# First expert's rows by one-hot products instead of an indirect transfer and transposes

## The chip, the cores and the metric

One core of one Trainium2 chip runs the whole program. The metric is the device time of one execution in microseconds (us). The kernel before takes 1440.48 us, the median of three runs (1439.84 to 1441.86).

## The reference, cut to what matters

Two layers of an encoder over 512 tokens of width 1024, all in float32. In each layer a token mixer (layer 0: convolution and a linear recurrence; layer 1: sliding-window attention) is followed by a mixture of experts: 16 experts, of which each token takes two, and each expert is a gated network of width 512.

```python
h = modulate(rmsnorm(x, norm_ffn_g[l]), sh2, sc2)        # per channel: scale and shift
x = x + g2[:, None, :] * grouped_moe(h, router_w, router_bias, ...)

# grouped_moe: sigmoid scores, best group of four experts, top two in it;
# the tokens of each expert are laid into blocks of 128 rows, absent rows are zero
xs = hpad[slot_tok].reshape(n_blocks, DISPATCH_BLOCK, D)
yb = (silu(xb @ w_gate[e]) * (xb @ w_up[e])) @ w_down[e]  # for every block
out = zeros.at[slot_tok].add(yb * slot_w[:, None])
```

## The kernel before, in words

The layer's tokens stand as four tiles of 128 rows. `experts(l)`, which each engine has in its own version, does the whole mixture of layer l. In the order of time:

**Routing.** For each tile the residual is added, the rows are normalized (`xnorm[s]`, 128 tokens by 1024 channels, kept in SBUF: `mod_ring` in layer 0, `x_norm` in layer 1, since s = 2l + 1), ScalarE's queue stores them to the DRAM tensor `xn_rows` (L818), and logits, scores and choices follow (`choose`). TensorE then counts ranks (L1740, L1742). From these VectorE makes the places:

- `place_first` (L1281 to L1291): the place of each token in expert 0's block, as a one-hot `first_hot` (128 tokens by 128 places, four tiles). TensorE multiplies it with a column of token numbers (L1747) and VectorE turns the sum into the first column of `slot_tok`, the list of the tokens of each block.
- `route` (L1293 to L1327): the same for all other blocks, by a chain of small VectorE instructions, eight products on TensorE (L1752) and two instructions for the remaining columns of `slot_tok` (L1325, L1326).

**Gathers.** GpSimd's queue fetches each block's rows from `xn_rows` by an indirect transfer into one of two buffers `xs` (L637 for experts 0 and 1, L644 for the others, always two experts ahead; the buffer is free when `xs_turned` has counted its transposes).

**Expert 0's entry.** `turn_xs` makes eight transposes of 128x128 into PSUM banks 0 and 1 (L1757); the stride in the gathered rows puts channels kt, kt + 8, ... on the partitions. `xst` takes them out with the layer's scale and shift, half on ScalarE (L833, L836), half on VectorE (L1401, L1404), and splits them into a high and a low part (VectorE, L1407).

**The expert loop.** For each expert TensorE makes 24 gate products (`split_product`, L1771: high times high, high times low and low times high part of the weights, 128x512 in fp32r, three for each of eight slices), the down product of the expert before (L1782, plain f32), the transposes of the next expert's rows (L1757), and 24 up products (L1771). Meanwhile ScalarE copies the high part of the weights (`high`, L804), VectorE subtracts it for the low part (`low`, L1377), and SyncE's queue refills the weight buffers (`refill`), each as soon as `gate_done`, `up_done` or `down_done` frees it. Weights come in slabs of 2 MB; two experts' slabs are loaded ahead of the loop. Blocks beyond the sixteenth, from experts with more than 128 tokens, run after the loop in the same way but one after the other (L1762).

Order is written out by hand: every engine runs its instructions in the order of its program, and semaphores order the engines. On VectorE the order is `place_first`, `route`, `xst(0)`, the low part of expert 0's up weights, `route_rest` (information for the extra blocks, combine weights), the low part of expert 1's gate weights, `xst(1)`. On TensorE it is L1747, L1752, the transposes of expert 0, its gate products, the transposes of expert 1 (L1813, behind a wait for `xs_filled[1]`), its up products. The gate weights of expert 0 are split during routing.

Of the kernel before, what the change touches and what calls it, by code (L numbers as in the profile page):

```python
# [92 lines left out]
def build(nc, ctx, a, out):  # L93
    def small(name, shape, dt=F32):
        return ctx.enter_context(nc.sbuf_tensor(name, shape, dt))
# [54 lines left out]
    first_hot = R_r[:, 12, :].rearrange("p (t n) -> p t n", n=P)  # L150
# [31 lines left out]
    tok_pair = small("token_id_pair", [P, TT, 2], F32R)  # L182
# [71 lines left out]
    xs_turned, xst_act, xst_dve = sem("xs_turned"), sem("xst_act"), sem("xst_dve")  # L254
    high_ready, low_ready = [sem("gate_high"), sem("up_high")], [sem("gate_low"), sem("up_low")]
# [82 lines left out]
    LAST = 4 * 7 + AV_LAG  # L338
    QK_BANK = [0, 1, 2, 3, 4, 5, 0, 1] + [2, 4, 5, 6, 7, 6, 7, 6]
# [242 lines left out]
    def _(gp):  # L582
# [46 lines left out]
        def gathers(l):  # L629
# [3 lines left out]
            gp.wait_ge(slots_ready, 2 * l + 1)  # L633
# [14 lines left out]
            gather_first(0, xs_filled[0])  # L648
            gp.wait_ge(slots_ready, 2 * l + 2)
# [51 lines left out]
    def _(act):  # L701
# [93 lines left out]
        def experts(l):  # L795
# [29 lines left out]
            def xst(e, par, first=False):  # L825

                if not first:
                    act.wait_ge(up_done, e + (e0 - 1))
                if first and par:
                    act.wait_ge(route_ready, l + 1)  # L830
                act.wait_ge(xs_turned, e + (e0 + 1))
                for kt in range(4):
                    ins = act.activation(xsT[par][:, kt, :], ps[:, 0, kt * P:(kt + 1) * P], ACT.Identity, bias=AB[:, s, 1, kt:kt + 1], scale=AB[:, s, 0, kt:kt + 1])  # L833
                ins.then_inc(xst_act, 1)
                act.wait_ge(xst_act, e + (e0 + 1))
                act.activation(xs_high[l][par][:, 0:4, :], xsT[par][:, 0:4, :], ACT.Copy).then_inc(xs_high_ready, 1)  # L836
# [124 lines left out]
    def _(v):  # L961
# [277 lines left out]
        link(v.tensor_copy(tok_pair[:, :, :], tok1[:, :].unsqueeze(2).to_broadcast([P, TT, 2])))  # L1239
# [41 lines left out]
        def place_first(l):  # L1281
# [5 lines left out]
            v.wait_ge(slots_summed, 2 * l + 1)  # L1287
            found = ps[:, 2, 0:1]
            link(ts(empty[:, 0:1], found, 0.0, float(NO_TOKEN), ALU.is_equal, ALU.mult))
            stt(slot_tok[:, 0:1], found, -1.0, empty[:, 0:1], ALU.add, ALU.add).then_inc(slots_ready, 1)  # L1290
            v.wait_ge(slots_ready, 2 * l + 1)  # L1291

        def route(l):  # L1293
# [29 lines left out]
            v.wait_ge(slots_summed, 2 * l + 2)  # L1323
            slots = ps[:, 2, 1:WIDE]
            link(ts(empty[:, 1:WIDE], slots, 0.0, float(NO_TOKEN), ALU.is_equal, ALU.mult))  # L1325
            stt(slot_tok[:, 1:WIDE], slots, -1.0, empty[:, 1:WIDE], ALU.add, ALU.add).then_inc(slots_ready, 1)  # L1326
            v.wait_ge(slots_ready, 2 * l + 2)  # L1327
# [21 lines left out]
        def experts(l):  # L1349
# [46 lines left out]
            def xst(e, par, first=False):  # L1396
                if not first:
                    v.wait_ge(up_done, e + (e0 - 1))
                v.wait_ge(xs_turned, e + (e0 + 1))
                for kt in range(4, KT):  # L1400
                    ins = ts(xsT[par][:, kt, :], ps[:, 1, (kt - 4) * P:(kt - 3) * P], AB[:, s, 0, kt:kt + 1], AB[:, s, 1, kt:kt + 1], ALU.mult, ALU.add)  # L1401
# [35 lines left out]
            xst(0, 0, True)  # L1437
            step(0, 0, first=True)
# [159 lines left out]
    def _(pe):  # L1598
# [106 lines left out]
        def experts(l):  # L1705
# [40 lines left out]
            for t in range(TT):  # L1746
                ins = pe.matmul(ps[:, 2, 0:2], first_hot[:, t, :], tok_pair[:, t, :], start=(t == 0), stop=(t == TT - 1))  # L1747
            ins.then_inc(slots_summed, 1)

            pe.wait_ge(place_ready, 2 * l + 2)  # L1750
            for i in range(2 * TT):
                ins = pe.matmul(ps[:, 2, 0:WIDE], place_hot[:, i, :], block_tok[:, i, :], start=(i == 0), stop=(i == 2 * TT - 1))  # L1752
# [43 lines left out]
            def step(e, par, turn, first=0, last=False):  # L1796
# [13 lines left out]
                if not last:  # L1810

                    pe.wait_ge(xs_filled[1 - par], (turn + par) * 16 + (16 + (NE // 2) * l * 16))
                    turn_xs(1 - par, xs_turned)  # L1813
# [3 lines left out]
            pe.wait_ge(xs_filled[0], (NE // 2) * l * 16 + 16)  # L1817
            turn_xs(0, xs_turned)
# [166 lines left out]
```

## Time and profile before

| | us |
|---|---|
| median of 3 runs | 1440.48 |
| the profiled execution | 1440.28 |
| its span | 1438.5 |
| TensorE (PE) busy | 1267.1 (88%) |
| VectorE (DVE) busy | 945.9 (66%) |
| ScalarE (ACT) busy | 592.0 (41%) |
| GpSimd (POOL) busy | 169.3 (12%) |

Mean granted TensorE clock 0.945 of 2.4 GHz; it has two levels, 1.00 (2.4 GHz) and 0.50 (1.2 GHz). Expert 0's first product starts at about 316 us in layer 0 and at about 1034 us in layer 1. The span is the time on the core from the first to the last instruction; the execution's own time is 1.8 us longer. Times of rows are counted from the start of the span. Matmuls are pipelined and their ends are modelled: the time that one costs in a row of many is the distance of the starts, not its own duration. PEld is the load of the stationary operand, DVEq or POOLq an engine's sequencer. In a chain of waits each piece is what released the next.

### The profile page before, as it was taken

The page shows a single profiled execution, that of the slowest core. Times are in us where ns is not written, and L with a number is a line of the kernel's source. Part 1 is how long each engine was busy: PE and PEld are TensorE (multiplying, and loading weights), DVE is VectorE, ACT ScalarE, POOL GpSimd, SP SyncE. Part 2 cuts the span into 40 slices and gives each one's busy share as a digit, 9 for nine tenths or more (in the row PEclk, how much of TensorE's full clock was granted, in tenths as well). Part 3 has the DMA queues.
Part 4 walks back from the last instruction along what each step waited for, and adds up shares of the span by engine and source line. Part 5 has one row for each costly group of instructions (what it writes and reads, how often), then busy time and mean ns, then how long its engine had stood idle before and what let it go on. Part 6 is the DMA issues. An engine that isn't in the chain of part 4 may idle for free.

```text
span 1438.5 us, 14181 instructions
## 1 busy us (share of the span) xinstructions
PE 1267.1 (88%) x4821; PEld 813.9 (57%) x4821; DVE 945.9 (66%) x1336; ACT 592.0 (41%) x774; POOL 169.3 (12%) x177
## 2 busy tenths in 40 slices
PE   2979899948999999983899999999489999999881
PEld 2434344546666667741788854467466666667430
DVE  8468985566777777713866588856667777777114
ACT  3246200335555555502422157734255555554001
POOL 6100000010000000002000047710110000000002
PEclk9999999959999999997899999999599999999996
DMA  9984575047999999883375230023679999998445
GB/s 354 375 283 124 198 256 212 30 146 273 372 363 369 373 372 375 307 334 122 127 282 185 88 117 1 1 74 127 241 289 374 377 366 365 378 363 310 146 181 190
DMA packets 79615, 353.12 MB, mean 245 GB/s; under 512 B 12696, under 2 KB 12880, under 8 KB 70608
## 3 DMA queue, kind: packets, MB, share of 16 engines
q1 hardware_dynamic: 67680, 327.28, 61.7%
q0 software_dynamic: 8352, 20.46, 3.9%
q10 hardware_dynamic: 3536, 4.79, 0.9%
q8 instruction: 26, 0.43, 0.1%
q14 instruction: 21, 0.17, 0.0%
HBM read 334.15 MB, written 28.31 MB: 252 GB/s over the span
## 4 chain that ended last, share of the span: by engine, by line
PE 74%; DVE 12%; SPq 5%; DMA 4%; ACT 2%; issue 2%; POOL 1%; DVEq 0%; ACTq 0%; POOLq 0%
PE ps L1771 24%; PE ps L1782 17%; PE ps L1870 8%; PE ps L1691 4%; PE ps L1762 3%; PE ps L1658 3%; PE ps L1698 2%; PE ps L1757 2%; DVE scratch L974 2%; PE ps L1914 2%; PE ps L1942 2%; SPq L398 2%; PE ps L1928 2%; DMA mod_ring<-in_mod_w_dram 1%; PE ps L1621 1%
## 5 line engine op out<-in xcount | busy, mean ns | idle before, releaser
L1782 PE MATMUL ps<-slab_ring,scratch 128*128 128x512 f32 x560 | 246.5, 593 | 3.4 <-ACT scratch L882 2.1
L1771 PE MATMUL ps<-slab_ring_r,gate_rows_r 128*128 128x512 f32 x512 | 202.4, 395 | 0.0
L1782 PEld LDWEIGHTS ps<-slab_ring,scratch 128*128 128x128 f32 x560 | 105.8, 190 | 124.2 <-issue 117.3
L1377 DVE TENSOR_TENSOR slab_ring_r<-slab_ring,h_t_r 128x2048 fp32r<-128x2048 f32 x64 | 143.9, 2287 | 17.2 <-ACT h_t_r L804 17.1
L1658 PE MATMUL ps<-h_t,slab_ring 128*128 128x512 f32 x320 | 141.2, 600 | 0.0
L1870 PE MATMUL ps<-slab_ring_r 128*128 128x512 f32 x384 | 121.2, 397 | 2.7 <-DVE h_t_r L1031 2.7
L1771 PE MATMUL ps<-h_t_r,gate_rows_r 128*128 128x512 f32 x256 | 106.4, 415 | 14.8 <-DVE scratch_r L1407 7.6
L804 ACT ACTIVATE h_t_r<-slab_ring 128x2048 fp32r<-128x2048 f32 x64 | 118.6, 1901 | 0.0
L1771 PEld LDWEIGHTS ps<-slab_ring_r,gate_rows_r 128*128 128x128 f32 x512 | 98.4, 192 | 19.4 <-issue 0.5
L1658 PEld LDWEIGHTS ps<-h_t,slab_ring 128*128 128x128 f32 x320 | 61.8, 194 | 77.8 <-issue 77.2
L833 ACT ACTIVATE scratch<-ps,mod_ab 128x128 f32<-128x128 f32 x128 | 48.1, 456 | 136.0 <-PE ps L1757 136.0
L1771 PE MATMUL ps<-h_t_r,scratch_r 128*128 128x512 f32 x256 | 103.0, 402 | 0.0
L1377 DVE TENSOR_TENSOR slab_ring_r<-slab_ring,x_norm_r 128x2048 fp32r<-128x2048 f32 x32 | 73.2, 2292 | 42.1 <-ACT x_norm_r L804 42.1
L1377 DVE TENSOR_TENSOR slab_ring_r<-slab_ring,mod_ring_r 128x2048 fp32r<-128x2048 f32 x32 | 73.2, 2292 | 41.3 <-ACT mod_ring_r L804 41.3
L696 POOL TENSOR_SCALAR mod_ring<-mod_ring,row_rcp 128x512 f32<-128x512 f32 x48 | 76.9, 1614 | 185.5 <-DVE row_rcp L1554 185.4
L1870 PEld LDWEIGHTS ps<-slab_ring_r 128*128 128x128 f32 x384 | 72.6, 190 | 20.0 <-issue 2.9
L1411 DVE TENSOR_TENSOR scratch<-ps,gate_rows 128x512 f32<-128x512 f32 x70 | 45.1, 686 | 53.9 <-PE ps L1782 52.9
L804 ACT ACTIVATE mod_ring_r<-slab_ring 128x2048 fp32r<-128x2048 f32 x32 | 61.1, 1912 | 46.8 <-PE ps L1771 46.6
L804 ACT ACTIVATE x_norm_r<-slab_ring 128x2048 fp32r<-128x2048 f32 x32 | 61.1, 1911 | 46.8 <-PE ps L1771 46.6
L1870 PE MATMUL ps<-slab_ring_r,h_t_r 128*128 128x512 f32 x192 | 75.3, 392 | 0.0
L1771 PEld LDWEIGHTS ps<-h_t_r,gate_rows_r 128*128 128x128 f32 x256 | 50.1, 196 | 25.8 <-issue 16.4
L974 DVE SCALAR_TENSOR_TENSOR scratch<-slab_ring,c_silu,scratch 128x1024 f32<-128x1024 f32 x42 | 59.9, 1426 | 3.9 <-DMA slab_ring<-in_mod_w_dram 2.6
(318 smaller groups left out, 2065.2 us busy)
## 6 DMA issues: line engine op xcount, KB each, us to landing
slab_ring<-in_expert_w_gate_dram SPq DMA_DIRECT2D x35, 2048.0 KB, 10.0
slab_ring<-in_expert_w_up_dram SPq DMA_DIRECT2D x35, 2048.0 KB, 10.4
slab_ring<-in_expert_w_down_dram SPq DMA_DIRECT2D x35, 2048.0 KB, 10.4
mod_ring<-in_mod_w_dram SPq DMA_DIRECT2D x48, 512.0 KB, 4.6
y_rows<-scratch SPq DMA_DIRECT2D x35, 512.0 KB, 10.8
slab_ring<-in_mod_w_dram SPq DMA_DIRECT2D x32, 512.0 KB, 4.6
slab_ring<-in_w_qkv_dram SPq DMA_DIRECT2D x6, 2048.0 KB, 11.3
slab_ring<-in_w_in_ab_dram SPq DMA_DIRECT2D x5, 2048.0 KB, 18.0
```

The source lines that it names most:

```text
L696: gp.tensor_scalar(prob[n % 8], prob[n % 8], rsum[:, n:n + 1], None, ALU.mult).then_inc(scaled_pool, 1)
L804: act.activation(top, w, ACT.Copy).then_inc(high_ready[c], 1)
L833: ins = act.activation(xsT[par][:, kt, :], ps[:, 0, kt * P:(kt + 1) * P], ACT.Identity, bias=AB[:, s, 1, kt:kt + 1], scale=AB[:, s, 0, kt: ...
L974: ins = stt(dest, w, cs[:, m:m + 1], dest, ALU.mult, ALU.add)
L1377: tt_(rest, w, top.bitcast(F32), ALU.subtract).then_inc(low_ready[c], 1)
L1411: ins = tt_(buf[:, h * HALF:h * HALF + HALF], ps[:, 5 + h, :], G[:, 2 * l + 1, h * HALF:h * HALF + HALF], ALU.mult)
L1658: ins = pe.matmul(ps[:, z_bank(t), :], slab(("in", g))[:, kt, j * P:(j + 1) * P], HT[:, kt, :], start=(kt == 0), stop=(kt == KT - 1))
L1691: ins = pe.matmul(ps[:, 2 * t + half, :], mixT[:, kt, cut], slab(("out", half))[:, kt, :], start=(i == 0), stop=(i == KT - 1))
L1762: ins = pe.matmul(ps[:, bank, :], xsT[0][:, kt, :], w[:, kt, :], start=(kt == 0), stop=(kt == KT - 1))
L1771: ins = pe.matmul(ps[:, bank, :], x, w, start=(kt == 0 and i == 0), stop=(kt == KT - 1 and i == 2))
L1782: ins = pe.matmul(ps[:, 5 + h, :], hidT[:, f, :], w[:, 2 * f + h, :], start=(f == 0), stop=(f == FT - 1))
L1870: ins = pe.matmul(ps[:, i % 6, :], x[:, kt, cut], y[:, k, :], start=(kt == 0 and n == 0), stop=(kt == KT - 1 and n == 2))
```

## The change

The rows of expert 0, already transposed, are made by products of the normalized rows with the one-hot of places: for each of the eight slices of channels four products (one for each tile of tokens, summed in PSUM), 32 in all, into banks 4 and 5. The stationary operand is `xnorm[s][:, t, kt:D:KT]`, with a stride of 8 elements, the moving one `first_hot[:, t, :]`. The indirect transfer and the eight transposes for expert 0 are gone, and so are the first column of the slots, its four products and VectorE's two instructions for it. `first_hot` is f32 instead of fp32r. The 32 products stand on TensorE where the four were, ahead of the eight slot products, which now go to bank 3. `xst` of expert 0 waits for `first_rows`, ScalarE's half after 16 products and VectorE's after 32. The two instructions that form the other columns of `slot_tok`, with their wait, move on VectorE from the end of `route` to behind `xst(0)` (`find_slots`); the gather of expert 1 waits for them. As `turn_xs(0)` is gone, TensorE raises `xs_turned` by itself once after the slot products, so that the gather of expert 2 into `xs[0]` may follow.

```diff
--- before.py
+++ after.py
@@ -147,7 +147,7 @@
     block_tok = R_r[:, 11, 0:2 * TT * WIDE].rearrange("p (a b) -> p a b", b=WIDE)
     XT = [R[:, 8 + 2 * i:10 + 2 * i, :].rearrange("p a (b n) -> p (a b) n", n=P) for i in range(2)]
     rw_scaled, rw_shift = (R[:, 12, i * P:(i + 1) * P].rearrange("p (k e) -> p k e", e=NE) for i in range(2))
-    first_hot = R_r[:, 12, :].rearrange("p (t n) -> p t n", n=P)
+    first_hot = R[:, 12, :].rearrange("p (t n) -> p t n", n=P)
     comb = [[XN[:, t, :] for t in range(TT)],
             [modr[:, 2 * t:2 * t + 2, :].rearrange("p a n -> p (a n)") for t in range(TT)]]
 
@@ -630,7 +631,7 @@
             e0 = l * NE
             gp.wait_ge(xn_ready, 4 * (2 * l + 2))
             link(gp.memset(R[:, 0:4, :], 0.0))
-            gp.wait_ge(slots_ready, 2 * l + 1)
+            gp.wait_ge(slots_ready, l + 1)
             gp.wait_ge(xn_stored, 16 * TT * (l + 1))
 
             def gather_first(buf, done):
@@ -645,8 +646,6 @@
                                       in_offset=bass.IndirectOffsetOnAxis(ap=idx[buf][:, 0:1], axis=0),
                                       bounds_check=S - 1, oob_is_err=False).then_inc(done, 16)
 
-            gather_first(0, xs_filled[0])
-            gp.wait_ge(slots_ready, 2 * l + 2)
             gather_first(1, xs_filled[1])
             with gp.Fori(0, NE // 2 - 1) as i:
                 link.enter_loop(i, 0, 2)
@@ -828,9 +827,13 @@
                     act.wait_ge(up_done, e + (e0 - 1))
                 if first and par:
                     act.wait_ge(route_ready, l + 1)
-                act.wait_ge(xs_turned, e + (e0 + 1))
+                if first and not par:
+                    act.wait_ge(first_rows, 2 * l + 1)
+                else:
+                    act.wait_ge(xs_turned, e + (e0 + 1))
+                bank = FIRST_BANK if first and not par else 0
                 for kt in range(4):
-                    ins = act.activation(xsT[par][:, kt, :], ps[:, 0, kt * P:(kt + 1) * P], ACT.Identity, bias=AB[:, s, 1, kt:kt + 1], scale=AB[:, s, 0, kt:kt + 1])
+                    ins = act.activation(xsT[par][:, kt, :], ps[:, bank, kt * P:(kt + 1) * P], ACT.Identity, bias=AB[:, s, 1, kt:kt + 1], scale=AB[:, s, 0, kt:kt + 1])
                 ins.then_inc(xst_act, 1)
                 act.wait_ge(xst_act, e + (e0 + 1))
                 act.activation(xs_high[l][par][:, 0:4, :], xsT[par][:, 0:4, :], ACT.Copy).then_inc(xs_high_ready, 1)
@@ -1284,11 +1286,6 @@
             link(stt(first_rank[:, :], hot[:, :, 0], -float(PAST), v3(ps[:, 1, 0:n])[:, :, 0], ALU.mult, ALU.add))
             link(ts(first_rank[:, :], first_rank[:, :], float(PAST), None, ALU.add))
             tt_(first_hot, p_id[:, :].unsqueeze(1).to_broadcast([P, TT, P]), first_rank[:, :].unsqueeze(2).to_broadcast([P, TT, P]), ALU.is_equal).then_inc(place_ready, 1)
-            v.wait_ge(slots_summed, 2 * l + 1)
-            found = ps[:, 2, 0:1]
-            link(ts(empty[:, 0:1], found, 0.0, float(NO_TOKEN), ALU.is_equal, ALU.mult))
-            stt(slot_tok[:, 0:1], found, -1.0, empty[:, 0:1], ALU.add, ALU.add).then_inc(slots_ready, 1)
-            v.wait_ge(slots_ready, 2 * l + 1)
 
         def route(l):
 
@@ -1320,11 +1317,14 @@
                 ins = tt_(block_tok[:, j * TT:(j + 1) * TT, :], at[:, j * TT:(j + 1) * TT, :], tok1[:, :].unsqueeze(2).to_broadcast([P, TT, WIDE]), ALU.mult)
             ins.then_inc(place_ready, 1)
             v.wait_ge(place_ready, 2 * l + 2)
-            v.wait_ge(slots_summed, 2 * l + 2)
-            slots = ps[:, 2, 1:WIDE]
+
+        def find_slots(l):
+
+            v.wait_ge(slots_summed, l + 1)
+            slots = ps[:, SLOT_BANK, 1:WIDE]
             link(ts(empty[:, 1:WIDE], slots, 0.0, float(NO_TOKEN), ALU.is_equal, ALU.mult))
             stt(slot_tok[:, 1:WIDE], slots, -1.0, empty[:, 1:WIDE], ALU.add, ALU.add).then_inc(slots_ready, 1)
-            v.wait_ge(slots_ready, 2 * l + 2)
+            v.wait_ge(slots_ready, l + 1)
 
         def route_rest(l):
 
@@ -1396,9 +1396,14 @@
             def xst(e, par, first=False):
                 if not first:
                     v.wait_ge(up_done, e + (e0 - 1))
-                v.wait_ge(xs_turned, e + (e0 + 1))
+                bank = 1
+                if first and not par:
+                    bank = FIRST_BANK + 1
+                    v.wait_ge(first_rows, 2 * l + 2)
+                else:
+                    v.wait_ge(xs_turned, e + (e0 + 1))
                 for kt in range(4, KT):
-                    ins = ts(xsT[par][:, kt, :], ps[:, 1, (kt - 4) * P:(kt - 3) * P], AB[:, s, 0, kt:kt + 1], AB[:, s, 1, kt:kt + 1], ALU.mult, ALU.add)
+                    ins = ts(xsT[par][:, kt, :], ps[:, bank, (kt - 4) * P:(kt - 3) * P], AB[:, s, 0, kt:kt + 1], AB[:, s, 1, kt:kt + 1], ALU.mult, ALU.add)
                 ins.then_inc(xst_turned, 1)
                 v.wait_ge(xst_turned, e + (e0 + 1))
                 v.tensor_copy(xs_high[l][par][:, 4:8, :], xsT[par][:, 4:8, :]).then_inc(xst_split, 1)
@@ -1435,6 +1440,7 @@
                 tt_(hid, ps[:, 3, :], sg, ALU.mult).then_inc(hid_ready, 1)
 
             xst(0, 0, True)
+            find_slots(l)
             step(0, 0, first=True)
             step(1, 1)
             step(2, 0)
@@ -1743,13 +1749,17 @@
             ins.then_inc(rank_ready, 1)
 
             pe.wait_ge(place_ready, 2 * l + 1)
-            for t in range(TT):
-                ins = pe.matmul(ps[:, 2, 0:2], first_hot[:, t, :], tok_pair[:, t, :], start=(t == 0), stop=(t == TT - 1))
-            ins.then_inc(slots_summed, 1)
+            pe.wait_ge(xn_ready, TT * s + TT)
+            for kt in range(KT):
+                for t in range(TT):
+                    ins = pe.matmul(ps[:, FIRST_BANK + kt // 4, (kt % 4) * P:(kt % 4 + 1) * P], xnorm[s][:, t, kt:D:KT], first_hot[:, t, :], start=(t == 0), stop=(t == TT - 1))
+                if kt == 3:
+                    ins.then_inc(first_rows, 1)
+            ins.then_inc(first_rows, 1)
 
             pe.wait_ge(place_ready, 2 * l + 2)
             for i in range(2 * TT):
-                ins = pe.matmul(ps[:, 2, 0:WIDE], place_hot[:, i, :], block_tok[:, i, :], start=(i == 0), stop=(i == 2 * TT - 1))
+                ins = pe.matmul(ps[:, SLOT_BANK, 0:WIDE], place_hot[:, i, :], block_tok[:, i, :], start=(i == 0), stop=(i == 2 * TT - 1))
             ins.then_inc(slots_summed, 1)
 
             def turn_xs(buf, done):
@@ -1809,13 +1819,15 @@
                     down_product(e - 1, 1 - par, prev_turn, first == 2)
                 if not last:
 
-                    pe.wait_ge(xs_filled[1 - par], (turn + par) * 16 + (16 + (NE // 2) * l * 16))
+                    if par == 0:
+                        pe.wait_ge(xs_filled[1], turn * 16 + (16 + (NE // 2) * l * 16))
+                    else:
+                        pe.wait_ge(xs_filled[0], turn * 16 + (16 + (NE // 2 - 1) * l * 16))
                     turn_xs(1 - par, xs_turned)
                 pe.wait_ge(low_ready[1], 2 * e + (2 * e0 + 2))
                 split_product(par, 1, 3, range(KT)).then_inc(up_done, 1)
 
-            pe.wait_ge(xs_filled[0], (NE // 2) * l * 16 + 16)
-            turn_xs(0, xs_turned)
+            pe.sem_inc(xs_turned, 1)
             step(0, 0, 0, first=1)
             step(1, 1, 0, first=2)
             with pe.Fori(1, NE // 2 - 1) as i:
```

Here `FIRST_BANK` is 4 and `SLOT_BANK` 3; `first_rows` is a new semaphore, and the tile `tok_pair` with the cast that filled it (L1239) is gone.

## Rows read from the trace of the kernel before

**Rows 1.** The page: the chain that ended last, shares by engine.
```profile
PE 74%; DVE 12%; SPq 5%; DMA 4%; ACT 2%; issue 2%; POOL 1%; DVEq 0%; ACTq 0%; POOLq 0%
```

**Rows 2.** Timeline of layer 0, 300 to 317 us: start us, us, engine, line, instruction.
```profile
301.73 1.01 PE L1747 MATMUL ps<-token_id_pair,scratch_r 128*128 128x2 f32 x4 [1.18 <-DVE scratch_r L1286]
...
303.17 0.17 DVE L1296 TENSOR_SCALAR scratch<-ps 128x16 f32<-128x16 f32 x1
...
308.81 1.88 PE L1752 MATMUL ps<-scratch_r 128*128 128x24 f32 x8 [6.06 <-DVE scratch_r L1320]
...
310.54 1.97 PE L1757 MATMUL ps<-ident,scratch 128*128 128x128 f32 x8
...
311.98 1.01 POOL L637 DMA_INDIRECT scratch<-xn_rows,slot_token  x1 [6.83 <-DVE slot_token L1326]
...
312.62 1.37 DVE L1401 TENSOR_SCALAR scratch<-ps,mod_ab 128x128 f32<-128x128 f32 x4 [1.42 <-PE ps L1757]
...
314.81 1.22 DVE L1407 TENSOR_TENSOR scratch_r<-scratch,gate_rows_r 128x1024 fp32r<-128x1024 f32 x1 [0.36 <-ACT gate_rows_r L836]
...
316.14 0.76 PE L1771 MATMUL ps<-h_t_r,gate_rows_r 128*128 128x512 f32 x1 [3.63 <-issue]
...
316.54 4.49 DVE L1377 TENSOR_TENSOR slab_ring_r<-slab_ring,x_norm_r 128x2048 fp32r<-128x2048 f32 x2 [0.51 <-ACT x_norm_r L804]
```

**Rows 3.** Chain of waits, layer 1, 1000 to 1060 us: start us, us, what.
```profile
1009.14 11.23 DMA xn_rows<-x_norm
...
1021.24 7.05 DMA scratch<-xn_rows,slot_token
...
1028.34 1.99 PE ps L1757 x8
...
1033.94 7.71 PE ps L1771 x24
```

**Rows 4.** Timeline of layer 1, the same product as at 301.73.
```profile
1016.97 1.01 PE L1747 MATMUL ps<-token_id_pair,scratch_r 128*128 128x2 f32 x4 [1.18 <-DVE scratch_r L1286]
```

**Rows 5.** Chain of waits, layer 0, 285 to 345 us: gate products of experts 0 and 1.
```profile
316.14 8.17 PE ps L1771 x24
...
334.43 4.58 PE ps L1771 x12
```

**Rows 6.** Chain of waits inside the expert loop, 345 to 600 us.
```profile
349.06 0.89 PE ps L1757 x8
349.94 8.20 PE ps L1771 x36
...
361.35 6.87 PE ps L1782 x16
```

**Rows 7.** Timeline of TensorE alone, three places: layer 0 before routing; logits; layer 1's start.
```profile
283.77 3.60 PE L1691 MATMUL ps<-slab_ring,x_norm 128*128 128x512 f32 x8
...
290.92 3.57 PE L1718 MATMUL ps<-scratch 128*128 128x16 f32 x16 [0.89 <-ACT scratch L811]
...
686.92 1.97 PE L1606 MATMUL ps<-ident,x_norm 128*128 128x128 f32 x8 [1.53 <-DVE x_norm L1010]
690.01 1.19 PE L1870 MATMUL ps<-slab_ring_r 128*128 128x512 f32 x2 [1.12 <-DVE h_t_r L1031]
```

**Rows 8.** Windows: us, busy (count) of PE, PEld, DVE, ACT, POOL, then PEclk, DMA, GB/s.
```profile
290.40:290.80 0.40, 0.00 (x0) 0.00 (x0) 0.40 (x2) 0.38 (x2) 0.00 (x0) 0.75 1.14 492
335.00:336.00 1.00, 1.00 (x4) 0.81 (x3) 1.00 (x1) 0.00 (x0) 0.00 (x0) 0.50 1.07 459
338.00:339.00 1.00, 1.00 (x6) 0.77 (x5) 0.00 (x0) 0.00 (x0) 0.00 (x0) 0.81 0.00 0
321.00:324.00 3.00, 3.00 (x14) 2.46 (x13) 2.23 (x12) 0.00 (x0) 0.00 (x0) 0.95 0.00 0
692.00:694.00 2.00, 2.00 (x8) 1.60 (x7) 1.93 (x6) 1.45 (x3) 0.00 (x0) 0.66 0.12 49
```

**Rows 9.** Landing times of the transfers that read slot_token.
```profile
DMA to landing us min/median/max: 3.4/4.6/7.1
```

More of the change, by code:

```diff
@@ L181, in build @@
     shift_row = small("router_shift_row", [P, NE])
-    tok_pair = small("token_id_pair", [P, TT, 2], F32R)
     first_rank = small("first_rank", [P, TT])
@@ L254, in build @@
     xs_turned, xst_act, xst_dve = sem("xs_turned"), sem("xst_act"), sem("xst_dve")
+    first_rows = sem("first_rows")
     high_ready, low_ready = [sem("gate_high"), sem("up_high")], [sem("gate_low"), sem("up_low")]
@@ L338, in build @@
     LAST = 4 * 7 + AV_LAG
+    FIRST_BANK, SLOT_BANK = 4, 3
     QK_BANK = [0, 1, 2, 3, 4, 5, 0, 1] + [2, 4, 5, 6, 7, 6, 7, 6]
@@ L1238, in _ @@
         n = TT * NE
-        link(v.tensor_copy(tok_pair[:, :, :], tok1[:, :].unsqueeze(2).to_broadcast([P, TT, 2])))
         sc, bia, o1, o2, t0, t1, t2, t3 = (rt[:, i * n:(i + 1) * n] for i in range(8))
```

## The prediction

> **What bounds the kernel now.** I read the page's chain first: TensorE carries 74% of it [rows 1]. In the expert loop it never pauses; every piece begins where the last one ended [rows 6]. The change leaves the loop's body alone, so it can only move the moment at which each of the two layers enters it. Next I read the timelines of both entries, from the routing to expert 0's first gate product.
>
> In layer 0 [rows 2] the one-hot of places is ready when the four products of L1747 start, at 301.73. VectorE waits for them, forms column 0 of the slots, and only at 303.17 begins `route`. The route ends with the eight slot products at 308.81; TensorE works in order, so expert 0's eight transposes follow at 310.54. They end at 312.51, VectorE takes its half at 312.62, and the gate products start at 316.14. The gather for expert 0 isn't in this: it was hidden behind the route. In layer 1 it is [rows 3]: a store of normalized rows takes 11.23 us, the gather issued behind it 7.05, and the transposes come at 1028.34, the gate products at 1033.94. The one-hot was ready at 1016.97 [rows 4].
>
> The clock matters too. Over 24 gate products TensorE needs 8.17 and 7.71 us [rows 5, 3], where 36 products in the loop take 8.20, or 0.228 each [rows 6], 5.5 for 24. So 2.7 and 2.2 us are lost to the lower clock at the two entries.
>
> **The change, part by part.**
>
> 1. Products for expert 0. Per layer 32 plain f32 products of 128x128 by 128x128 replace four products and eight transposes. No row has this form. The nearest are f32 transposes with the same strided stationary: 8 in 0.89 us, 0.111 each, at 2.4 GHz [rows 6], and 8 in 1.97, about 0.24, at 1.2 GHz [rows 7]; products with 16 columns show 16 in 3.57, 0.22 each [rows 7]. A plain f32 product of 512 columns takes 6.87/16 = 0.429 [rows 6]; a quarter of that is 0.107, no more than the transpose. I take 0.111 and 0.23. The lower bound is 0.107; the upper is a 128-column product that costs as much as a 512-column one, 0.43, and double that at half clock. The transposes are nearest, in shape and in stride, so I stay with them.
>
> 2. The clock while they run. They start at 1.2 GHz. Dense 512-column products got the full clock 5.2 us after their start (316.14 to 321.3: 0.95 granted in 321 to 324), 4.0 us (334.43 to 338.4) and 3.35 us (690.01 to 693.36) [rows 2, 5, 7, 8]. I take 4.3: 19 products in 4.3 us, 13 in 1.45, with the last one's drain 5.9 us. They end at 307.6 and 1022.9.
>
> By the Trainium skill (FP8 and Floating Point Precision, TensorE Precision Notes) true f32 is four passes through the array. The trace disagrees: its plain f32 product costs 0.429 against 0.228 for the split one, less than twice. With four passes of 128 columns at the two clocks, the products would end 3 us later in each layer.
>
> 3. VectorE without its wait. `route` starts at once, 1.44 us earlier, and ends at about 307.3 and 1022.5; TensorE's products end later, so they bind, by 0.3 us. VectorE's wait for the eight slot products disappears ahead of `xst`. They run beside `xst` and cost the path nothing; without this cover they would cost the 1.73 us between their start and that of the transposes [rows 2].
>
> 4. `xst`. Before, from the end of the transposes to the gate product, 316.14 - 312.51 = 3.63 us, of which 0.36 waits for ScalarE's copy [rows 2]. ScalarE now starts after half the products (first at about 305.5) and finishes first, so 3.27 remain. Gate products start at 310.9 and 1026.2: **5.2 and 7.7 us earlier**. All 24 gate products' other operands are ready: the low part of the gate weights is made before routing.
>
> 5. Clock at the gate products. The eight slot products end near 308.6, and 2.3 us of pause follow. The clock fell 3.2 us after the products that ended at 287.4 (three quarters granted in 290.4 to 290.8), with eight transposes between, and some 4.4 us after the end of expert 0's up products, which is 0.5 us into the next burst (0.50 in 335 to 336) [rows 7, 8]. So I expect it to fall about when the gate products start and to come back as for expert 1, whose first 12 took 4.58 us [rows 5] against 2.73: 1.85 lost instead of 2.7 and 2.2. **Gain 0.85 and 0.35.** The bounds are no fall, 2.7 and 2.2, and no gain, 0.
>
> 6. Moved: the other slots, now behind `xst`. Two small instructions, 0.4 us like column 0's pair between 302.74 and 303.17, stand ahead of the low part of the up weights. Queued behind them on VectorE are 4.49 us of that [rows 2] and the eleven small instructions of `route_rest`, by L1296's 0.17 and at most twice that some 2 to 3.5 us, so VectorE is free by 317.6 to 319.2. The next work for it, expert 1's gate weights, waits for ScalarE, which copies them only after the gate products (318.2) and its silu. Nothing is late. ScalarE makes the high part of the up weights earlier than now, so VectorE's 0.51 wait there goes too.
>
> 7. Moved: expert 1's gather. It is issued about 0.8 us after its slots, near 312, with 3.4 to 7.1 us to land [rows 9, 2], so by 319.1 at worst; TensorE wants it when the gate products end, at 318.2. Expert 1 starts 10.1 us after that (324.3 to 334.43), of which TensorE needs 1.04 for transposes and 5.5 for up products, so 3.5 us are free. Cost zero. In layer 1 it is issued at about 1027.2, as now. POOL has one indirect transfer less to issue; expert 2's can't pass expert 1's, since it stands behind it. No weight transfer moves in its order on SP; its refills follow the gate products and move with them.
>
> 8. PE's empty increment, the cast of L1239 that is gone, and f32 instead of fp32r in the one-hot: nothing, the same width is written.
>
> Sum: 5.2 + 7.7 + 0.85 + 0.35 = 14.1. The profiled execution took 1440.28 us, 0.2 less than the median 1440.48; 1440.28 - 14.1 = **1426.2**.
>
> **The rivals.**
>
> A, the clock stays high at the gate products. The pause of 2.3 us is shorter than each after which it was seen to fall. Against it: in layer 0 eight transposes in the pause didn't keep it up, and the eight slot products are as short. Both losses vanish, 2 x 1.85 = 3.7 us more: 1422.5.
>
> B, the clock doesn't rise during the 32 products. For it: 16 logit products in 3.57 us and two groups of eight transposes (the second ends at 688.9) ran at the low clock throughout [rows 7]. Against: each dense burst of true products with many columns in the rows brought it up, and the new ones run for 6 us without a pause. 32 x 0.235 = 7.5 us, gates at 312.5 and 1027.8, gain 3.6 + 6.1, nothing from the clock: 1430.6.
>
> C, load and stream don't overlap for 128 columns. 0.106 for the load (half of the logits' 0.22) and 0.107 for the stream make 0.213. 10 products in 4.3 us and 22 in 4.7 end at 310.7 and 1026.0; gates at 314.0 and 1029.2, gain 2.1 + 4.7 + 1.2 = 8.0: 1432.3. Four passes would come out at the same place.
>
> D, slower: TensorE becomes the bound of the entry, each product costing as much as one of 512 columns (item 1's upper bound). Five in 4.3 us and 27 x 0.43 = 11.6 end 16 us after the start, gates at 321.0 and 1036.2: 4.9 + 2.3 later, 1447.5. It decides from some 0.41 us a product: 11.1 and 13.7 us until the products would end as late as the path allows now, plus the clock, over 32. Every f32 row of 128 columns lies below, so it is unlikely.
>
> E, expert 1's gather lands late, as the store's 11.23 us did: at about 323.2, 1.5 us past the slack in each layer: 1429.2.
>
> That the change doesn't do what it says is small in layer 0: the transfer was hidden there, and what is gained is the wait, slots and transposes.
>
> **How the numbers follow.** Forecast 0.43, A 0.22, B 0.16, C 0.13, E 0.04, D 0.02. The range takes in A, B and C with the bounds of the clock: 1421.5 to 1433.0. About 0.2%, 2.9 us, is what a measurement of this kernel can tell from no change; all cases but D lie beyond it on the faster side. With something left for what is not seen: faster 0.95, same 0.03, slower 0.02.
>
> **What would show it.** Right: 32 products at 0.11 to 0.24 us starting at 301.7; L1296 within 0.1 us of L1286's end; the first gate product at 310 to 312 and 1025 to 1027.5; PE waiting for no transfer before expert 1; the loop's pieces unchanged (8.20 and 6.87). Wrong: a mean above 0.25 per product, a granted clock of 0.50 through all of them, a wait for the transfer into `xs[1]`, or an expert loop with pauses.

## The result and the profile after

The changed kernel takes 1449.92 us, the median of five runs (1448.04 to 1452.46), against 1441.15 us for the kernel before in the same series. The ratio is 1.0065 with a 95% interval of 1.0054 to 1.0075: **slower by 0.65%, where 1% faster was forecast**. A second series of five gave 1448.91 us and 1.0055 (1.0041 to 1.0069). In the series that timed v3 and b1, one execution of b1 and one of the kernel before took some 1740 us at a granted clock of 0.73; the ratios leave both out.

The page of the changed kernel, its busy times and its chain, beside [rows 1]:

```profile
PE 1291.1 (89%) x4925; PEld 836.9 (58%) x4925; DVE 944.4 (65%) x1331; ACT 592.6 (41%) x774; POOL 169.9 (12%) x175
...
PE 75%; DVE 12%; SPq 5%; DMA 2%; ACT 2%; issue 2%; POOL 1%; DVEq 0%; ACTq 0%; POOLq 0%
```

TensorE is 24 us busier (1267.1 before). Its timeline at layer 0's entry, the stretch that answers to [rows 2] (L1755 are the new products, L1762 the slot products, L1781 the gate products; L1288 makes the one-hot and L1293 is the first instruction of `route`):

```profile
304.09 0.69 DVE L1288 TENSOR_TENSOR scratch<-place_id,first_rank 128x512 f32<-128x512 f32 x1
304.70 0.17 DVE L1293 TENSOR_SCALAR scratch<-ps 128x16 f32<-128x16 f32 x1
...
304.84 15.54 PE L1755 MATMUL ps<-scratch,mod_ring 128*128 128x128 f32 x64 [1.18 <-DVE scratch L1288]
...
309.86 0.43 DVE L1317 TENSOR_TENSOR scratch_r<-scratch,token_id_plus 128x96 fp32r<-128x96 f32 x2
312.79 1.51 ACT L836 ACTIVATE scratch<-ps,mod_ab 128x128 f32<-128x128 f32 x4 [13.92 <-PE ps L1755]
...
320.13 1.04 PE L1762 MATMUL ps<-scratch_r 128*128 128x24 f32 x8
320.49 1.37 DVE L1406 TENSOR_SCALAR scratch<-ps,mod_ab 128x128 f32<-128x128 f32 x4 [10.20 <-PE ps L1755]
...
323.49 0.17 DVE L1325 TENSOR_SCALAR slot_empty<-ps 128x23 f32<-128x23 f32 x1
...
323.68 0.77 PE L1781 MATMUL ps<-h_t_r,gate_rows_r 128*128 128x512 f32 x1 [2.50 <-issue]
```

VectorE starts `route` at 304.70, at the moment at which the one-hot is ready, as the change meant, and ends it at 310.3. Then it stands still for 10.2 us: the 32 products run from 304.84 to 320.38. Everything behind them has the form that was forecast: the slot products in their cover, 3.30 us from the last product to the first gate product. In layer 1, the answer to [rows 3, 4], products and entry are the same to a hundredth:

```profile
1024.69 15.54 PE L1755 MATMUL ps<-scratch,x_norm 128*128 128x128 f32 x64 [1.18 <-DVE scratch L1288]
...
1043.54 0.77 PE L1781 MATMUL ps<-h_t_r,gate_rows_r 128*128 128x512 f32 x1 [2.51 <-issue]
```

The rows of line L1755 alone:

```profile
L1755 PEld LDWEIGHTS ps<-scratch,mod_ring x64: 312/336/338, 304.8 to 319.8; 128*128 128x128 f32 x64
L1755 PE MATMUL ps<-scratch,mod_ring x64: 342/402/604, 304.8 to 320.0; 128*128 128x128 f32 x64
```

The code writes 32 products a layer, and here are 64 matmuls. A plain f32 product is **two** records (rows of the trace), each with its own load. And a record costs 15.5/64 = 0.24 us whatever the clock does. The windows of the same stretch (us, busy time and count of PE, PEld, DVE, ACT, POOL, then PEclk, DMA, GB/s; a count takes in the records that a window's edge cuts, so it is higher than the window's length over the price of one):

```profile
306.00:308.00 2.00, 2.00 (x10) 2.00 (x10) 1.73 (x9) 0.00 (x0) 0.00 (x0) 0.50 0.00 0
308.00:310.00 2.00, 2.00 (x11) 2.00 (x10) 1.90 (x4) 0.00 (x0) 0.00 (x0) 0.79 0.00 0
318.00:320.00 2.00, 2.00 (x10) 2.00 (x10) 0.00 (x0) 1.84 (x2) 0.00 (x0) 1.00 0.00 0
320.00:321.00 1.00, 1.00 (x10) 1.00 (x9) 0.51 (x2) 0.00 (x0) 0.00 (x0) 1.00 0.00 0
322.00:323.00 1.00, 0.00 (x0) 0.00 (x0) 0.97 (x2) 0.00 (x0) 0.00 (x0) 0.75 0.00 0
323.00:324.00 1.00, 0.32 (x1) 0.35 (x2) 0.93 (x4) 0.00 (x0) 0.00 (x0) 0.50 0.00 0
```

The granted clock rises at 308.8 (0.79 over 308 to 310), 4.0 us after the start, and the ten records in each 2 us don't become more. The slot products right behind, plain records of 24 columns, run at some 0.11 us each. The clock falls at 322.5 (0.75 over 322 to 323), 1.3 us after the last slot product, while VectorE takes the rows out, so that the gate products begin at the lower clock again. In the chain they take 8.36 us; expert 1 follows at its old distance (316.14 to 334.43 before was 18.3, now 18.5):

```profile
323.68 8.36 PE ps L1781 x24
...
342.16 3.06 PE ps L1781 x8
```

The table has, for the kernels of this study except the control b1, the records that make expert 0's rows in a layer, the way from the first of them to the first gate product ("entry"), and from there to the transposes of expert 1 ("gate"), for layer 0 / layer 1, read from the starts in the timelines. Times are medians, or one run where a single one is marked.

| kernel | records | entry | gate | time |
|---|---|---|---|---|
| before | 4 + 8 | 14.41 / 16.97 | 7.99 / 7.53 | 1441.15 |
| changed | 64 | 18.84 / 18.85 | 8.18 / 8.34 | 1449.92 |
| r1, changed again | 64 | 18.86 / 18.83 | 7.54 / 7.94 | 1448.91 |
| u1, slots ahead | 64 | 20.08 / 20.34 | 6.95 / 7.26 | 1448.58 |
| e1, contiguous | 64 | 12.26 / 12.97 | 7.19 / 5.78 | 1432.08, one |
| v1, permuted rows | 64 | 13.52 / 12.16 | 8.38 / 7.19 | 1437.00 |
| e4, v3, one pass | 32 | 11.24 / 11.24 | 8.00 / 7.40 | 1431.42 |
| v2, permuted, one pass | 32 | 10.39 / 10.39 | 8.31 / 7.16 | 1432.29 |
| e2, transposes | 32 | 8.71 / 8.98 | 6.69 / 5.74 | 1421.94, one |
| e3, one tile | 16 | 8.67 / 8.67 | 7.50 / 8.12 | 1427.59, one |

(The entry and gate columns of "e4, v3" are e4's; its time is v3's.) Before to changed, the entries cost 4.4 + 1.9 and the gate products 0.2 + 0.8: 7.3 us of a measured 8.8 and 8.1. The profiled execution was the slowest of its five (span 12.2 us longer): its routing in layer 0 began 3.1 us later than before, and in r1 that start lies within 0.3 us of before (301.98 against 301.73). So that part is scatter between executions.

### The profile page after: what moved, and what is told of

The parts are those of the page before. It is cut to its first block, busy times and chain, and to the rows that moved or that the text cites. A ratio compares the mean times of both kernels' runs of the same rounds, so it can differ in the third digit from the quotient of the medians.

```text
span 1450.7 us, 14377 instructions
## 1 busy us (share of the span) xinstructions
PE 1291.1 (89%) x4925; PEld 836.9 (58%) x4925; DVE 944.4 (65%) x1331; ACT 592.6 (41%) x774; POOL 169.9 (12%) x175
## 4 chain that ended last, share of the span: by engine, by line
PE 75%; DVE 12%; SPq 5%; DMA 2%; ACT 2%; issue 2%; POOL 1%; DVEq 0%; ACTq 0%; POOLq 0%
PE ps L1781 24%; PE ps L1792 17%; PE ps L1882 8%; PE ps L1697 4%; PE ps L1772 3%; PE ps L1664 3%; PE ps L1704 2%; PE ps L1755 2%; DVE scratch L977 2%; SPq L399 2%; PE ps L1767 2%; PE ps L1926 2%; PE ps L1954 2%; PE ps L1940 2%; PE ps L1627 1%
## 5 line engine op out<-in xcount | busy, mean ns | idle before, releaser
L1781 PE MATMUL ps<-slab_ring_r,gate_rows_r 128*128 128x512 f32 x512 | 203.1, 397 | 0.0
L1377 DVE TENSOR_TENSOR slab_ring_r<-slab_ring,h_t_r 128x2048 fp32r<-128x2048 f32 x64 | 143.9, 2288 | 18.5 <-ACT h_t_r L803 18.4
L1781 PE MATMUL ps<-h_t_r,gate_rows_r 128*128 128x512 f32 x256 | 106.6, 417 | 12.6 <-DVE scratch_r L1412 7.6
L1781 PEld LDWEIGHTS ps<-slab_ring_r,gate_rows_r 128*128 128x128 f32 x512 | 98.5, 192 | 19.4 <-issue 0.5
L1781 PE MATMUL ps<-h_t_r,scratch_r 128*128 128x512 f32 x256 | 103.3, 403 | 0.0
L1781 PEld LDWEIGHTS ps<-h_t_r,gate_rows_r 128*128 128x128 f32 x256 | 50.0, 195 | 23.0 <-issue 13.5
## 6 DMA issues: line engine op xcount, KB each, us to landing
slab_ring<-in_expert_w_down_dram SPq DMA_DIRECT2D x35, 2048.0 KB, 10.2
```

The source lines that it names most:

```text
L1377: tt_(rest, w, top.bitcast(F32), ALU.subtract).then_inc(low_ready[c], 1)
L1781: ins = pe.matmul(ps[:, bank, :], x, w, start=(kt == 0 and i == 0), stop=(kt == KT - 1 and i == 2))
```

## The experiments

**e1, contiguous stationary.** Does the stride make the record dear?

```diff
-pe.matmul(..., xnorm[s][:, t, kt:D:KT], first_hot[:, t, :], ...)
+pe.matmul(..., xnorm[s][:, t, kt * P:(kt + 1) * P], first_hot[:, t, :], ...)
```

> The changed kernel with the stationary operand of the 32 products taken from 128 neighbouring columns instead of every eighth (it multiplies other channels, so expert 0's rows hold the wrong channels; the work is the same). Stride theory: each f32 product is two matmul records, and a record with a strided stationary costs 0.24 us at either clock, a contiguous one 0.23 at the low and 0.11 at the full clock; the clock rises about 4 us after the start, so the 64 records take about 9.2 us instead of 15.5, and the way from the first product to the first gate product 12.5 us instead of 18.85 in each layer, some 12 us less in all, about 1438. Rival, the stream or the accumulation of 128 columns sets the 0.24: nothing changes, 15.5 us and about 1450.

1432.08 us in one run, beside 1439.98 for the kernel before. The loads of L1755 in layer 0, and the windows around them:

```profile
L1755 PEld LDWEIGHTS ps<-scratch,mod_ring x64: 192/192/338, 303.3 to 311.9; 128*128 128x128 f32 x64
```

```profile
304.00:306.00 2.00, 2.00 (x11) 2.00 (x11) 1.76 (x8) 0.00 (x0) 0.00 (x0) 0.50 0.00 0
306.00:308.00 2.00, 2.00 (x18) 2.00 (x17) 1.83 (x6) 0.00 (x0) 0.00 (x0) 0.86 0.03 8
308.00:310.00 2.00, 2.00 (x21) 2.00 (x20) 0.70 (x3) 1.28 (x4) 0.00 (x0) 1.00 0.00 0
316.00:318.00 2.00, 2.00 (x8) 1.59 (x7) 2.00 (x1) 0.00 (x0) 1.30 (x1) 0.70 0.00 0
```

The same 64 records take 8.96 us instead of 15.54. Their load falls to 192 ns, and with the clock full a window of 2 us counts 21 records, not 10. For the products and the entry the stride theory's numbers came out (9.2 and 12.5 expected; 8.96 and 12.26 measured in layer 0, 9.66 and 12.97 in layer 1, where the clock rose later, 4.7 us after the start against 3.3); the rival, that the stream or accumulation of 128 columns sets 0.24, is refuted. The time came out 6 us below the 1438 expected. Beside r1 below, the gate products are 2.5 us shorter in all, and an extra block behind the loop takes 14.02 us instead of 15.71; neither was in the estimate, and the rest isn't resolved.

**e2, transposes.** What the prediction had priced, put in the place of the products.

```diff
-ins = pe.matmul(..., xnorm[s][:, t, kt:D:KT], first_hot[:, t, :], start=(t == 0), stop=(t == TT - 1))
+ins = pe.transpose(..., xnorm[s][:, t, kt:D:KT], ident[:, :])
```

> The changed kernel with 32 transposes (identity as the moving operand, the same strided stationary) in place of the 32 f32 products; expert 0's rows are the wrong ones. This is what the prediction priced. If the count of records was its error, there are 32 records here; at 0.11 after the clock has risen they take 5.9 us, at 0.23 throughout (earlier transposes never raised the clock) 7.5 us; the first gate product comes 9.3 to 10.8 us after the first record, and the time is 1426 to 1431. Rival, the stride costs 0.24 a record in transposes too: 7.7 us and no drop even when the clock is full.

1421.94 us in one run, 4 below what was expected at best. The loads in layer 0, then the chain behind the first gate products:

```profile
L1755 PEld LDWEIGHTS ps<-ident,mod_ring x32: 185/200/226, 303.2 to 308.2; 128*128 128x128 f32 x32
```

```profile
313.02 5.51 DMA scratch<-xn_rows,slot_token
...
318.57 1.16 PE ps L1767 x8
319.73 5.49 PE ps L1781 x24
...
327.71 2.30 PE ps L1781 x9
```

32 records, 5.41 us, with a stride and yet 0.11 each at the full clock: the same stationary operand is cheap in a transpose and dear in a true product. The entry is 8.71 us. The clock is still full at the gate products (5.74 us in layer 1; the 6.69 of layer 0 hold a wait, below), so it is the prediction's case A in its mechanism, and within a microsecond of that case's 1422.5. The chain also shows the gather of expert 1 landing after the gate products, TensorE waiting for it until 318.57, and expert 1's gate products at 327.71. That is 15.8 us after expert 0's at 311.88, and in layer 1, where nothing waited, it is 15.8 too (1018.11 to 1033.93): the wait of about a microsecond went into the slack.

**e3, one tile of four.** The dose: 16 records.

```diff
-for t in range(TT):
-    ins = pe.matmul(..., start=(t == 0), stop=(t == TT - 1))
+for t in range(1):
+    ins = pe.matmul(..., start=(t == 0), stop=True)
```

> The changed kernel with 8 products of the 32: only the first 128 tokens are looked through, so most of expert 0's rows are missing. 16 records at 0.24: 3.9 us. The products no longer bind; the first gate product comes where VectorE's route ends, about 5.4 us after the start of the products, plus 3.3 for taking the rows out, so 8.8 us instead of 18.85: 20 us less in all than the changed kernel, about 1430. If something other than these products delays the entry (code, the moved slots), it stays above 12 us.

1427.59 us in one run. Timeline of VectorE's last route instructions and what follows:

```profile
306.70 0.43 DVE L1317 TENSOR_TENSOR scratch_r<-scratch,token_id_plus 128x96 fp32r<-128x96 f32 x2
307.16 1.37 DVE L1406 TENSOR_SCALAR scratch<-ps,mod_ab 128x128 f32<-128x128 f32 x4
...
310.35 0.76 PE L1781 MATMUL ps<-h_t_r,gate_rows_r 128*128 128x512 f32 x1 [1.29 <-issue]
```

The products end before `route`, VectorE goes from L1317 straight into L1406, and the entry is 8.67 us. Nothing else in the changed entry delays it, neither code nor moved slots. The way of 8.67 us through VectorE is the floor of this order of work.

**e4, one pass.** One record a product, the stride kept. For this the normalized rows and the one-hot are written as fp32r, the type in which the split products take their operands and to which f32 values are rounded; so all experts' rows are rounded.

```diff
-first_hot = R[:, 12, :].rearrange("p (t n) -> p t n", n=P)
+first_hot = R_r[:, 12, :].rearrange("p (t n) -> p t n", n=P)
...
-ts(xnorm[s][:, t, :], X[:, t, :], r, None, ALU.mult)
+ts((xnorm_r if s % 2 else xnorm)[s][:, t, :], X[:, t, :], r, None, ALU.mult)
...
-pe.matmul(..., xnorm[s][:, t, kt:D:KT], ...)
+pe.matmul(..., xnorm_r[s][:, t, kt:D:KT], ...)
```

> The changed kernel with normalized rows and one-hot written as fp32r, so that each of the 32 products is one record instead of two; all experts' rows are rounded to fp32r. Stride theory in its strict form (0.24 for every strided true product): 32 records in 7.7 us, the first gate product 11 us after the first record instead of 18.85, about 1434. If the stride costs only in the two-record f32 form: 5.9 us, 9.3 us, about 1431. Rival (stream or accumulation of 128 columns sets it): also half of 15.5.

1431.28 us. The loads, and two of four windows, which all read alike:

```profile
L1756 PEld LDWEIGHTS ps<-scratch_r,mod_ring_r x32: 313/337/339, 302.7 to 310.1; 128*128 128x128 f32 x32
```

```profile
304.00:306.00 2.00, 2.00 (x10) 2.00 (x10) 1.72 (x9) 0.00 (x0) 0.00 (x0) 0.50 0.00 0
...
310.00:312.00 2.00, 2.00 (x11) 2.00 (x10) 1.29 (x4) 2.00 (x2) 0.00 (x0) 0.50 0.00 0
```

32 records in 7.93 us, 0.25 each: the strict form of the theory in its numbers (7.7 and 11 expected, 7.93 and 11.24 measured). The total doesn't tell the cases apart: 1434 was expected for this one, 1431 for the other. It isn't settled whether the stride holds fp32r records at 0.24 when the clock is full, as the clock never rose here.

**r1, the changed kernel again.**

> The changed kernel unaltered, on the chip and in the hour of the next three, to see how much of its 9 us belongs to the two entries. The entries are 4.4 and 1.9 us longer than before and the gate products there 0.2 and 0.6: 7.1 us. If the rest (the profiled run began layer 0's routing 3.1 us later, before anything that the change touches) is the scatter of this kernel's runs, the median stands 7 to 9 us above the kernel before; if the change delays the program's start as well, 10 to 12.

1448.91 us, 8.1 above before, with the entries as in the first profile. By the table entries and gate products account for 4.45 + 1.86 - 0.45 + 0.41 = 6.3 of it. Most of the other 1.8 us stands in layer 1's second extra block: its 32 gate and up records took 14.02 us in the profile before, at a granted clock of 1.00 throughout, and 15.71 in both profiles of the changed kernel, in r1 with 0.57 granted over the first 4 us. In the first one's chain:

```profile
1393.69 15.71 PE ps L1772 x32
```

**v1, rows permuted.** e1 with the channels in their places.

```diff
-ts(xnorm[s][:, t, :], X[:, t, :], r, None, ALU.mult)
+ts(xnorm[s][:, t, :].rearrange("p (k c) -> p k c", c=P), X[:, t, :].rearrange("p (c k) -> p k c", k=KT), r, None, ALU.mult)   # s odd
...
-xs[buf][:, kt:D:KT], ident[:, :]
+xs[buf][:, kt * P:(kt + 1) * P], ident[:, :]
...
-xnorm[s][:, t, kt:D:KT], first_hot[:, t, :]
+xnorm[s][:, t, kt * P:(kt + 1) * P], first_hot[:, t, :]
```

> The stationary operand contiguous and the result right: VectorE writes the normalized rows with their channels already in the order that the products and the transposes want (one instruction a tile with a strided input), the store and the gathers carry that order, and transposes and products take 128 neighbouring columns. Stride theory: 64 records in 9.0 us as in e1, the first gate product 12.3 us after the first record, and at most 0.5 us more on the last tile's VectorE instruction: 1432 to 1434, faster than before by 6 to 8. If the gain of e1 came from its other data, the products take 15.5 us again and it stays near 1450.

1437.00 us over eight runs, ratio 0.9968 (0.9958 to 0.9979): faster than before, by less than expected. The products take 10.21 and 8.87 us, as the clock rose 5.9 us after their start in layer 0 and 3.1 in layer 1. The reordering costs VectorE 0.4 us a tile (L1014 writes the permuted rows, L1016 the others), and from expert 1's gate products in layer 0 to the first product of layer 1 it now takes 684.0 us against 682.5 before. The clock took the rest of what is lost against e1: gate products of 8.38 and 7.19 us against 7.19 and 5.78, and 15.71 against 14.02 in the second extra block. (The profiled execution, 1439.79 us, was the slowest of the eight.) VectorE's instructions:

```profile
L1014 DVE TENSOR_SCALAR mod_ring<-x_res,stats 128x1024 f32<-128x1024 f32 x4 | 4.6, 1156 | 0.1
...
L1016 DVE TENSOR_SCALAR x_norm<-x_res,stats 128x1024 f32<-128x1024 f32 x4 | 3.0, 754 | 0.1
```

**v2, permuted and one pass.** v1 with e4's fp32r rows and one-hot.

```diff
-ts(xnorm[s][:, t, :].rearrange("p (k c) -> p k c", c=P), ...)
+ts(xnorm_r[s][:, t, :].rearrange("p (k c) -> p k c", c=P), ...)
...
-pe.matmul(..., xnorm[s][:, t, kt * P:(kt + 1) * P], first_hot[:, t, :], ...)
+pe.matmul(..., xnorm_r[s][:, t, kt * P:(kt + 1) * P], first_hot[:, t, :], ...)   # first_hot in fp32r
```

> As v1, with rows and one-hot in fp32r (rows rounded), so 32 contiguous records instead of 64. If stride and record count are the two whole causes, these 32 cost what the 32 transposes of e2 cost, 5.2 us with the clock rising on the way, first gate product 8.7 to 9.3 us after the first record, 1422 to 1425. If the clock stays down as it did in e4: 7.4 us, 10.8 us, about 1430.

1432.29 us, ratio 0.9945 (0.9931 to 0.9958). The second case came true, so stride and record count are not the two whole causes: the clock is a third. The loads, one of the windows, which read alike from 303 to 315, and the timeline of TensorE:

```profile
L1759 PEld LDWEIGHTS ps<-scratch_r,mod_ring_r x32: 286/333/333, 303.3 to 309.9; 128*128 128x128 f32 x32
```

```profile
305.00:307.00 2.00, 2.00 (x12) 2.00 (x11) 1.76 (x8) 0.00 (x0) 0.00 (x0) 0.50 0.00 0
```

```profile
303.29 7.09 PE L1759 MATMUL ps<-scratch_r,mod_ring_r 128*128 128x128 f32 x32 [1.18 <-DVE scratch_r L1292]
310.18 1.82 PE L1766 MATMUL ps<-scratch_r 128*128 128x24 f32 x8
313.68 0.77 PE L1785 MATMUL ps<-h_t_r,gate_rows_r 128*128 128x512 f32 x1 [1.68 <-issue]
```

32 contiguous records at 0.22: the low clock throughout. At that clock the stride matters little (7.09 against e4's 7.93), and the reordering on VectorE buys nothing in the total over e4 (v3 below).

**u1, slots ahead.** One part of the change undone.

```diff
+find_slots(l)
 xst(0, 0, True)
-find_slots(l)
```

> The changed kernel with one part undone: VectorE forms the other experts' slots ahead of taking out expert 0's rows, as before. Priced from the trace: it waits for the eight slot products (0.8 us after the last of the 32) and then makes two instructions of 0.2, so the first gate product comes 1.3 us later in each layer, 2.6 in all. Rival, the move was worth nothing: within 0.5 us of the changed kernel.

1448.58 us, 0.3 below r1. VectorE in layer 0:

```profile
318.16 0.18 DVE L1325 TENSOR_SCALAR slot_empty<-ps 128x23 f32<-128x23 f32 x1 [11.02 <-PE ps L1762]
318.38 0.18 DVE L1326 SCALAR_TENSOR_TENSOR slot_token<-ps,slot_empty 128x23 int32<-128x23 f32 x1
318.60 1.36 DVE L1406 TENSOR_SCALAR scratch<-ps,mod_ab 128x128 f32<-128x128 f32 x4
```

The entries are 1.2 and 1.5 us longer, as priced, but the time is where the rival put it, within 0.5 us of the changed kernel. The gate products came out 0.6 and 0.7 us shorter than r1's, and the second extra block took 14.02 us instead of 15.71, at a granted clock of 1.00. So the move is worth its microsecond at the entry, and no gain of it is shown in the total.

**v3, e4 timed.**

> The kernel of e4 again (strided rows and one-hot in fp32r, 32 records, all experts' rows rounded), timed over several runs, because it beat both kernels in one. Entries of 11.24 us as there, 7.6 us a layer shorter than the changed kernel's 18.85: 1431 to 1434, about 0.994 of the kernel before. If e4's one time was a lucky run, its ratio comes out above 0.997.

1431.42 us over five runs (1429.22 to 1433.34), ratio 0.9933 (0.9920 to 0.9946). With v2, whose interval overlaps, it is the best of the kernels with all their work: 9.3 us below before, 17.5 below r1 of the other series. Its price is the rounding of the experts' rows.

**b1, control.** The kernel before with v1's first two edits and no products.

> Control for v1 and v2: the kernel before with its gather and its transposes, only with the normalized rows written in the permuted order and contiguous transposes. If the gain of v1 lies in the products at the entry, this gains nothing: the transposes stay at 0.11 us each in the loop, and four longer VectorE instructions a layer (1.16 against 0.75 us) cost up to 1.6 us a layer, so 1441 to 1444. If contiguous transposes in the loop were what made v1 faster, it is 1437 or less.

1442.01 us over twelve runs, ratio 1.0006 (0.9997 to 1.0015). The order of the rows alone gains nothing, so v1's gain comes from the entry.

## Why the prediction was wrong

**Step 1 failed, the price of the products: 0.111 and 0.23 us each were taken, 0.486 was measured. It failed first in how rows were counted.** The prediction read "8 in 0.89" for transposes, "16 in 3.57" for the logits and "6.87/16 = 0.429" for a plain f32 product of 512 columns, and called each record a product. The counts of the kernel before say otherwise. First the transposes, by their line, then the down products, from the page:

```profile
L1757 PE MATMUL ps<-ident,scratch x280: 272/274/477, 310.5 to 1381.0; 128*128 128x128 f32 x140
```

```profile
L1782 PE MATMUL ps<-slab_ring,scratch 128*128 128x512 f32 x560 | 246.5, 593 | 3.4 <-ACT scratch L882 2.1
```

Thirty-five blocks go through each line (16 experts in two layers and three extra blocks), with eight transposes and eight down products each: 280 and 560. A transpose is one record, a true f32 product two. The plain f32 product of 512 columns therefore costs 0.86 us, 3.8 times the split one's 0.228. The Trainium skill (FP8 and Floating Point Precision, TensorE Precision Notes) says that true f32 takes four passes through the array, and this trace agrees with it. The prediction said that the trace disagreed, because it divided by records. Dividing the count of a row by what the code issues would have caught it.

**The second half of the step was the stride.** The nearest row by shape was the transpose; the nearest by operation and stride was there too, but not read: `mod_reduce` (L1624) multiplies `acc[:, kt:D:KT]` in plain f32, with one column. Its rows, by line and in the timeline, with a window:

```profile
L1624 PEld LDWEIGHTS ps<-ones,scratch x32: 312/335/336, 21.5 to 39.1; 128*128 128x128 f32 x32
L1624 PE MATMUL ps<-ones,scratch x32: 367/376/377, 21.5 to 39.2; 128*128 128x1 f32 x32
```

```profile
21.52 3.94 PE L1624 MATMUL ps<-ones,scratch 128*128 128x1 f32 x16 [21.52 <-DVEq L978]
```

```profile
22.00:24.00 2.00, 2.00 (x10) 2.00 (x10) 1.01 (x2) 1.99 (x4) 1.85 (x3) 1.00 1.04 388
```

Eight products, 16 records, 3.94 us: 0.246 each, with the load at 335 ns, what the new products show (336). And this is at a granted clock of 1.00. One tile's logits, also plain f32 in 16 records but with a contiguous stationary operand, ran at the same clock in layer 0, at 0.115 each, their loads at 192 ns:

```profile
260.43 1.85 PE L1718 MATMUL ps<-scratch 128*128 128x16 f32 x16
```

The two rows together had the price of the stride, and that the full clock doesn't lower it, before anything ran. 64 times 0.246 is 15.7, against a measured 15.54. With it the entries would have come out at 15.7 + 3.3 = 19.0 us, 4.6 and 2.0 longer than before, and the forecast at about 1447.

The bound of that step, a product that costs as much as one of 512 columns, was meant to be far out and carried case D, with a chance of 0.02 and 1447.5 us. Measured is 0.486 a product, above the 0.41 from which D was said to decide. D had right that TensorE's products become the bound of the entry. That its time came so close is luck: it added five products at 0.86 and 27 at 0.43 to 16 us, and neither the columns nor the clock set the cost, but records and stride. Cases B (every record at its low-clock price) and C (twice the work a product) were each half of it, and the prediction never let the two meet.

**The other steps.** Step 2: the clock rose 4.0 us after the start (4.4 in layer 1), 4.3 were taken, but it bought nothing on strided records. Step 3: VectorE began `route` 1.5 us earlier, as said; TensorE then bound the path by 10 us instead of 0.3. Step 4: 3.27 forecast, 3.30 measured. Step 5: the fall was expected about when the gate products start; it came 1.2 us ahead, and with 8.36 us in the chain instead of some 7.3 the gain of 0.85 was a loss of 0.2; in layer 1 it came 0.8 us ahead, and the gain of 0.35 was a loss of 0.8. The prediction had placed it by falls 3.2 and 4.4 us after the end of a burst, and here it came 1.3 and 1.7 us after the slot products; why is open. In e1 it came at 316.8, 1.3 us after the start of the gate products, and layer 0's gate time was 7.19. Steps 6 and 7: nothing waited for the moved slots, and the gather cost nothing, even in e2, where it landed a microsecond late. With one-record transposes in the place of the products, e2 ran at 1421.9, inside the range of 1421.5 to 1433.0 but 4 below the forecast of 1426.2: step 1 is what put the time outside, and step 5 missed there too, as no fall came before or during the gate products.

## What to carry to other kernels

Before a row prices a new instruction, divide its count by the operations that the code issues: here one line of f32 code was two records, one transpose one. Then look for a row with the same operation and the same access pattern, even if its other shape is far off; a strided stationary operand doubled the price of a plain f32 record at the full clock (0.24 against 0.11) and left a transpose alone. And read the clock beside each row, so that a price is known for both levels. Where a product only selects rows and their rounding is acceptable, write its operands as fp32r: that halved the time of the entry's products (15.54 to 7.93 us) and turned a loss of 0.65% into a gain of 0.67%.

## What had not been expected of the hardware

- A strided f32 record costs 0.24 us at a granted clock of 0.50 and of 1.00; a contiguous one 0.22 and 0.11. So the page's PEclk line can be full while the products run as if it weren't. What in the load makes the difference was not tried.
- 32 transposes brought the clock up (e2: 3.4 and 4.0 us after their start, 32 records in 5.41 us, where 32 at 0.23 are over 7), though two groups of eight before [rows 7] hadn't. 64 f32 records did too, 4.0 and 4.4 us after their start in the changed kernel, 3.3 and 4.7 in e1. 32 fp32r products with eight slot products behind them, 9.6 us of unbroken work in e4 and 8.7 in v2, did not in either layer. Which property of the work decides that stays open; an estimate from e1's 0.11 a record is that v2's entry would have come near e2's if it had risen there.
- The second extra block of layer 1 takes 14.0 or 15.7 us for the same 32 records, by where the clock's steps fall. This is as large as the effects of single parts here, and u1 shows that a part worth 2.7 us at the entries can vanish in it and in the gate products' clock.
